# A ring of five in-place weight slots in a two-layer hybrid encoder, with every low part on VectorE and the memory's key and value units moved to the boundaries

## The chip, the cores and the metric

## The reference, cut to what matters

```python
for l in range(2):                       # x is (256, 1024), mem is (256, 1024), all float32
    x = layer_norm(ALPHA * x + 0.5 * swiglu(x, w_gate[l, 0], w_up[l, 0], w_down[l, 0]))   # d_ff 2816
    x = layer_norm(ALPHA * x + hybrid_mix(x))     # concat(diff attention, mLSTM, S5) @ w_out
    q, (k, v) = x @ wq[l], split(mem @ wkv[l])    # 4 heads of 256
    x = layer_norm(ALPHA * x + softmax(q @ k.T / 16) @ v @ wo[l])
    x = layer_norm(ALPHA * x + 0.5 * swiglu(x, w_gate[l, 1], w_up[l, 1], w_down[l, 1]))
```

The keys and values of the memory depend on `mem` and the weights alone, not on x.

## The kernel before

**Split products.** Each large product is made of three: both factors are split into a high part (`XH`, `WH`: a rounded copy, made by ScalarE) and a low part (`XL`, `WL`: the full number less the high part, made by VectorE's `low` or by GpSimd), and `prod` adds high x high, high x low and low x high into PSUM. 512 token-by-column results are 24 matmuls of 512 columns per unit, or 48 of 256.

**Units.** The weights come in units of 1 MB (128 partitions x 2048 float32), 99 a layer, in a fixed order: 33 for the first FFN (for each of 11 blocks two units of gate and up, one of down), K0, the mix's projections (DQ, SU, MQ, MK, DK, DV, MM), K1, K2, four units of V in the middle of the mix, five of `w_out` (the first two are half units), K3, four of `wq`, five of `wo` (two of them half), 33 for the second FFN. K and V are units of `wkv`, applied to the memory. A unit passes through slot u % 3 of three tiles, `RAW`, `WH` and `WL`. SyncE loads `RAW` (two transfers of 512 KB) when the low part of unit u - 3 is made (`load`); ScalarE's `split` waits for the load and until TensorE has used unit u - 3; VectorE's `split`, or for five units a layer (DQ1, the last two of `w_out`, the first of `wq`, the second of the second FFN) GpSimd's `split`, makes the low part; TensorE's `unit_ready` waits for that.

**Order.** Every engine's order is written out by hand, so that a low part stands at a fixed place between other steps of its engine and waits there. In the FFN, `step(j)` of ScalarE and VectorE makes H of block j high and low and the parts of three further units. In the mix, VectorE does the convolution and the S5 scans (`conv`, `s5_turn_in`), the masks and maxima (`diff_max`), the sums of the two softmaxes (`diff_combine`), the mLSTM sums and statistics (`mlstm_sums`, `mlstm_stats`) and the head norms (`diff_norm`); ScalarE the exponentials (`diff_exp`) and the copies out of PSUM (`diff_turned` copies the turned probabilities to AT). TensorE's memory units stand between the small matmuls of the heads.

**Boundaries.** Behind each of the four parts of a layer stands a boundary: VectorE's `norm_center` and `norm_scale` (a chain of small steps, `rsqrt`, in between), TensorE's `turn_x` turns the new X, ScalarE makes it high, VectorE low (`turned`). TensorE has one memory unit to do at the first boundary (K0) and at the second (K3), none at the third and fourth. At the first, third and fourth it starts the next product with tile 0 (128 tokens) alone; at the second, before the cross attention, it waits for both tiles.

**Loops.** The two layers are a hardware loop on each engine, and so are the blocks of the second FFN.

## Time and profile before

| | |
|---|---|
| median of 3 runs | 1379.81 us (1379.19 to 1384.34) |
| profiled execution | 1379.35 us |
| its span | 1377.7 us |
| busy: TensorE, VectorE, ScalarE, GpSimd | 92%, 62%, 42%, 17% |
| mean granted clock | 0.954 |
| transfers | 219.74 MB, 160 GB/s |

The span is the time from the first to the last instruction of the program; what lies around it is 1.65 us. Times in the rows count from the span's start. A row of the timeline is start, duration, engine, line, operation, output <- input, count, and in brackets the idle time of the engine ahead of it with what ended it. PE is TensorE, DVE VectorE, ACT ScalarE, POOL GpSimd.

### The profile page before, as it was taken

The page shows a single profiled execution, that of the slowest core. Times are in us where ns is not written, and L with a number is a line of the kernel's source. Part 1 is how long each engine was busy: PE and PEld are TensorE (multiplying, and loading weights), DVE is VectorE, ACT ScalarE, POOL GpSimd, SP SyncE. Part 2 cuts the span into 40 slices and gives each one's busy share as a digit, 9 for nine tenths or more (in the row PEclk, how much of TensorE's full clock was granted, in tenths as well). Part 3 has the DMA queues.
Part 4 walks back from the last instruction along what each step waited for, and adds up shares of the span by engine and source line. Part 5 has one row for each costly group of instructions (what it writes and reads, how often), then busy time and mean ns, then how long its engine had stood idle before and what let it go on. Part 6 is the DMA issues. An engine that isn't in the chain of part 4 may idle for free.

```text
span 1377.7 us, 18681 instructions
## 1 busy us (share of the span) xinstructions
PE 1267.3 (92%) x6376; PEld 1063.4 (77%) x6376; DVE 847.5 (62%) x1232; ACT 582.4 (42%) x659; POOL 232.1 (17%) x176
## 2 busy tenths in 40 slices
PE   5999997999978979999889999979997899899996
PEld 5877886978758868888768788868786797688885
DVE  4678556694875474445566774647758746645554
ACT  5443443435634444444354334434255244444442
POOL 0027001473040010000000440033902200000000
PEclk8999998999989989999989999989998899899999
DMA  8755553425234345555356555532433343455550
GB/s 274 269 174 183 188 177 105 135 97 178 92 123 152 128 145 196 192 193 183 124 202 208 183 184 183 183 123 93 153 107 123 108 153 123 155 190 192 192 185 30
DMA packets 151442, 219.74 MB, mean 160 GB/s; under 512 B 6720, under 2 KB 119488, under 8 KB 151104
## 3 DMA queue, kind: packets, MB, share of 16 engines
q1 hardware_dynamic: 148352, 205.61, 44.1%
q0 software_dynamic: 2736, 12.05, 2.4%
q8 instruction: 44, 0.72, 0.2%
q10 hardware_dynamic: 272, 1.05, 0.2%
q14 instruction: 38, 0.31, 0.1%
HBM read 217.63 MB, written 1.05 MB: 159 GB/s over the span
## 4 chain that ended last, share of the span: by engine, by line
PE 73%; DVE 18%; issue 6%; ACT 1%; DMA 1%; DVEq 0%; SPq 0%; ACTq 0%
PE PS L427 22%; PE PS L429 22%; PE PS L428 22%; DVE SM L1326 2%; DVE WL L1307 1%; DVE XG L1349 1%; PE PS L458 1%; DVE X L1343 1%; PE PS L496 1%; DVE ZS L1487 1%; DVE COUT L1499 1%; PE PS L900 1%; PE PS L924 1%; ACT WH L976 1%; DMA RAW<-in_ffn_w_up 1%
## 5 line engine op out<-in xcount | busy, mean ns | idle before, releaser
L1307 DVE TENSOR_TENSOR WL<-RAW,WH 128x2048 fp32r<-128x2048 f32 (+1 forms) x188 | 423.7, 2256 | 274.6 <-ACT WH L976 274.1
L976 ACT ACTIVATE WH<-RAW 128x2048 fp32r<-128x2048 f32 (+1 forms) x198 | 371.2, 1877 | 181.0 <-PE PS L429 178.8
L427 PE MATMUL PS<-WH,XH 128*128 128x512 f32 x832 | 337.6, 406 | 26.7 <-DVE XL L1307 20.2
L428 PE MATMUL PS<-WL,XH 128*128 128x512 f32 x832 | 330.4, 397 | 0.0
L429 PE MATMUL PS<-WH,XL 128*128 128x512 f32 x832 | 330.2, 397 | 0.0
L427 PEld LDWEIGHTS PS<-WH,XH 128*128 128x128 f32 x832 | 160.1, 192 | 62.3 <-issue 22.8
L429 PEld LDWEIGHTS PS<-WH,XL 128*128 128x128 f32 x832 | 159.9, 192 | 34.8
L428 PEld LDWEIGHTS PS<-WL,XH 128*128 128x128 f32 x832 | 160.6, 193 | 31.8
L427 PE MATMUL PS<-WH,HH 128*128 128x512 f32 x352 | 138.0, 392 | 4.0 <-DVE HL L1307 4.0
L429 PE MATMUL PS<-WH,HL 128*128 128x512 f32 x352 | 137.1, 389 | 0.0
L428 PE MATMUL PS<-WL,HH 128*128 128x512 f32 x352 | 137.0, 389 | 0.0
L1875 POOL TENSOR_TENSOR WL<-RAW,WH 128x2048 fp32r<-128x2048 f32 x10 | 45.6, 4561 | 342.8 <-ACT WH L976 342.8
L976 ACT ACTIVATE HH<-PS 128x512 fp32r<-128x512 f32 x44 | 26.3, 597 | 154.4 <-PE PS L458 154.4
L427 PEld LDWEIGHTS PS<-WH,HH 128*128 128x128 f32 x352 | 66.1, 188 | 19.9 <-issue 6.5
L1058 ACT ACTIVATE SG<-PS 128x256 f32<-128x256 f32 x88 | 33.8, 384 | 109.6 <-PE PS L429 109.5
L429 PEld LDWEIGHTS PS<-WH,HL 128*128 128x128 f32 x352 | 66.1, 188 | 13.9
L428 PEld LDWEIGHTS PS<-WL,HH 128*128 128x128 f32 x352 | 66.1, 188 | 13.4
L1307 DVE TENSOR_TENSOR HL<-PS,HH 128x512 fp32r<-128x512 f32 x44 | 30.4, 690 | 73.1 <-ACT HH L976 72.4
L427 PE MATMUL PS<-XH,WH 128*128 128x256 f32 x224 | 66.8, 298 | 3.2 <-DVE XL L1307 3.2
L428 PE MATMUL PS<-XL,WH 128*128 128x256 f32 x224 | 65.6, 293 | 0.0
L429 PE MATMUL PS<-XH,WL 128*128 128x256 f32 x224 | 65.3, 292 | 0.0
L496 PE MATMUL PS<-kst,X 128*128 128x128 f32 x128 | 24.4, 358 | 35.4 <-DVE X L1360 35.4
(308 smaller groups left out, 1796.0 us busy)
## 6 DMA issues: line engine op xcount, KB each, us to landing
RAW<-in_ffn_w_gate SPq DMA_DIRECT2D x88, 512.0 KB, 3.7
RAW<-in_ffn_w_up SPq DMA_DIRECT2D x88, 512.0 KB, 4.7
RAW<-in_ffn_w_down SPq DMA_DIRECT2D x88, 512.0 KB, 3.9
RAW<-in_w_in SPq DMA_DIRECT2D x44, 512.0 KB, 4.2
RAW<-in_xattn_wkv SPq DMA_DIRECT2D x32, 512.0 KB, 4.3
RAW<-in_xattn_wq SPq DMA_DIRECT2D x16, 512.0 KB, 4.3
RAW<-in_w_out SPq DMA_DIRECT2D x12, 512.0 KB, 3.9
RAW<-in_xattn_wo SPq DMA_DIRECT2D x12, 512.0 KB, 3.7
```

Source lines behind the costliest of these rows:

```text
L427: nc.tensor.matmul(out_ap, sh, mh, start=first, stop=False)
L428: nc.tensor.matmul(out_ap, sh, ml, start=False, stop=False)
L429: return nc.tensor.matmul(out_ap, sl, mh, start=False, stop=last)
L458: mm = nc.tensor.transpose(PS[:, 6, fc * SEQ + t * P:fc * SEQ + t * P + P], HB[:, t, fc * P:fc * P + P], ident)
L496: mm = nc.tensor.transpose(PS[:, 4 + 2 * t + half, i * P:i * P + P], X[:, t, c * P:c * P + P], ident)
L900: mm = nc.tensor.matmul(PS[:, h, t * SEQ:t * SEQ + SEQ], QX[:, 2 * h + c, t * P:t * P + P], KT[:, 2 * h + c, :], start=(c == 0), stop=(c = ...
L924: mm = nc.tensor.matmul(PS[:, 6 + h % 2, dc * SEQ:dc * SEQ + SEQ], V[:, mt, (2 * h + dc) * P:(2 * h + dc + 1) * P], XPT[:, h % 2, mt, :], ...
L976: return nc.scalar.activation(dst, src, ACT.Copy)
L1058: nc.scalar.activation(SG[:, t, :], PS[:, 4 + t, 0:FB], ACT.Silu).then_inc(sg_done.sem, 1)
L1307: return v.tensor_tensor(dst, full, hi.bitcast(F32), ALU.subtract)
L1326: ins = v.scalar_tensor_tensor(dst, a, 1.5, dst, ALU.add, ALU.mult)
L1875: g.tensor_tensor(WL[s][:, :], RAW[s][:, :], WH[s][:, :].bitcast(F32), ALU.subtract)\
```

## The change

- **Ring.** Five slots instead of three. A slot has `RAW` and `WH`; `WL` lies in the place of `RAW`, so the low part is written over the loaded unit. SyncE's load of unit u waits until TensorE has used unit u - 5. ScalarE's high part waits for the load alone. All low parts are on VectorE; GpSimd has none.
- **Place.** `split()` on ScalarE and VectorE takes the next unit of the order each time. Through the FFN and the mix it is one unit further on at the same place than before.
- **Memory units.** V units are eight column blocks of 256 with all 1024 rows (48 matmuls of 256 columns) instead of halves of the rows with 512 columns. `FILL` says where they are done: two at a boundary, four in the middle of layer 0's mix, none in layer 1's. Layer 1's K units are done at layer 0's last two boundaries.
- **Boundary.** Both tiles are centred and then scaled together everywhere. VectorE makes tile 0 of the turned X low, then the next weight's low part, then tile 1's.
- **Loops** are written out. The parameters come in four transfers instead of one, some of them in places that are free at that time; small rows of the gates lie in other tiles, and the heads' row maxima are spread by a column of the identity with stride 0 instead of a table.

```diff
-RING = 3
+RING = 5
+FILL = {("mix", 0): [(0, "K", 0), (0, "K", 1)],
+        ("mid", 0): [(0, "K", 2), (0, "K", 3), (0, "V", 0), (0, "V", 1)],
+        ("xattn", 0): [(0, "V", 2), (0, "V", 3)],
+        ("ffn2", 0): [(1, "K", 0), (1, "K", 1)],
+        ("next", 0): [(1, "K", 2), (1, "K", 3)],
+        ("mix", 1): [(1, "V", 0), (1, "V", 1)],
+        ("mid", 1): [],
+        ("xattn", 1): [(1, "V", 2), (1, "V", 3)],
+        ("ffn2", 1): [],
+        ("next", 1): []}
...
+EARLY = {(0, l): 2 for l in range(DEPTH)} | {(1, l): 2 for l in range(DEPTH)} | {(2, 0): 3, (2, 1): 1, (3, 0): 3, (3, 1): 0}
...
+        slots = [place(f"RAW{s}", [P, 2048], F32) for s in range(RING)]
+        RAW = [slot for slot, _ in slots]
+        WL = [sb(f"WL{s}", [P, 2048], F32R, at) for s, (_, at) in enumerate(slots)]
         WH = [sb(f"WH{s}", [P, 2048], F32R) for s in range(RING)]
-        WL = [sb(f"WL{s}", [P, 2048], F32R) for s in range(RING)]
...
-            def load(l, u, j, first, second):
-
-                sp.wait_ge(split_lo.sem, split_lo.at(l, u - RING + 1 + 3 * j))
+            def load(u, first, second):
+
+                if u >= RING:
+                    sp.wait_ge(unit_used.sem, u - RING + 1)
...
+            def memory_unit(key, b):
+
+                u = UNIT[key]
+                if key[1] == "K":
+                    form_b(u, b, MH, ML)
+                    return
+                unit_ready(u)
...
+                for t in range(TT):
+                    tok = slice(t * P, t * P + P)
+                    for c in range(KC):
+                        mm = prod(PS[:, b, t * 256:t * 256 + 256], MH[:, c, tok], ML[:, c, tok],
+                                  wh[:, c, :], wl[:, c, :], c == 0, c == KC - 1)
+                mm.then_inc(unit_used.sem, 1)
+
+            def fill(where, l):
+
+                for i, key in enumerate(FILL[where, l]):
+                    memory_unit(key, 7 - i)
...
# ScalarE
-                act.wait_ge(raw_loaded[s].sem, raw_loaded[s].at(l, 32 * (u // RING + 1) + 32 * j))
-                act.wait_ge(unit_used.sem, unit_used.at(l, u - RING + 1 + 3 * j))
+                act.wait_ge(raw_loaded[s].sem, 32 * (u // RING + 1))
                 copy(WH[s][:, 0:n], RAW[s][:, 0:n]).then_inc(split_hi.sem, 1)
...
+            def boundary(l, n):
...
                 square(l, n, 0)
                 square(l, n, 1)
...
+                fill_out(where, l, 0)
+                split()
...
+                turned(nl, nn, 0)
+                fill_out(where, l, 1)
+                turned(nl, nn, 1)
+                for i in range(EARLY[n, l] - 1):
+                    split()
...
# VectorE
+            def boundary(l, n):
...
+                norm_center(l, n, 0, last)
+                norm_center(l, n, 1, last)
+                norm_scale(l, n, 0, 2)
...
+                turned(nl, nn, 0)
+                split()
+                turned(nl, nn, 1)
+                for i in range(EARLY[n, l] - 1):
+                    split()
...
# VectorE, mix: the end, from the last decay_scores
                 diff_max(l, 4)
                 diff_max(l, 5)
...
                     CH[:, 6:8, :].rearrange("p f (k s) -> p f k s", s=2)).then_inc(c_lo.sem, 1)
+                split()
                 mlstm_sums(l)
-                split(l, U_WOUT[1], half=True)
                 diff_combine(l, 2)
+                split()
                 mlstm_stats(l)
                 diff_max(l, 6)
                 diff_max(l, 7)
-                split(l, U_WOUT[2])
+                split()
                 diff_combine(l, 3)
                 cat_low(l, 0, 4, 7)
                 diff_norm(l, 0)
                 cat_low(l, 1, 0, 4)
+                split()
                 diff_norm(l, 1)
                 cat_low(l, 2, 2, 5)
-                split(l, U_K[3])
+                split()
+                split()
...
# ScalarE, mix: the end
                 diff_exp(l, 4)
                 diff_exp(l, 5)
-                split(l, U_WOUT[1], half=True)
-                kv_out(l, 6)
-                kv_out(l, 7)
+                split()
+                if FILL["mid", l]:
+                    kv_out(FILL["mid", l][3], 0)
                 diff_evac(l, 1)
                 diff_turned(l, 2)
-                split(l, U_WOUT[2])
+                split()
                 diff_exp(l, 6)
                 diff_exp(l, 7)
-                split(l, U_WOUT[3])
+                split()
                 cat_high(l, 0, 4, 7)
...
# VectorE, end of the attention
                 output(3)
-                split(l, U_WO + 4)
-                split(l, U_FFN[1])
+                for i in range(4):
+                    split()
```

## Rows read from the trace of the kernel before

**Rows 1.** The page: busy time of the engines, and groups of instructions.
```profile
PE 1267.3 (92%) x6376; PEld 1063.4 (77%) x6376; DVE 847.5 (62%) x1232; ACT 582.4 (42%) x659; POOL 232.1 (17%) x176
...
L976 ACT ACTIVATE WH<-RAW 128x2048 fp32r<-128x2048 f32 (+1 forms) x198 | 371.2, 1877 | 181.0 <-PE PS L429 178.8
...
L1875 POOL TENSOR_TENSOR WL<-RAW,WH 128x2048 fp32r<-128x2048 f32 x10 | 45.6, 4561 | 342.8 <-ACT WH L976 342.8
```

**Rows 2.** Waits of TensorE, longest first: total us, times, longest.
```profile
PE PS L496 <- DVE X L1360: 35.4, 7, 6.5
PE PS L427 <- DVE XL L1307: 23.4, 8, 8.0
PE PS L724 <- DVE ES L1601: 13.4, 2, 6.7
...
PE PS L427 <- DVE HL L1307: 4.0, 4, 1.1
```

**Rows 3.** Groups of VectorE by form: busy us, mean ns, idle before.
```profile
L1307 DVE TENSOR_TENSOR WL<-RAW,WH 128x2048 fp32r<-128x2048 f32 x180 | 413.9, 2302 | 271.6 <-ACT WH L976 271.3
...
L1307 DVE TENSOR_TENSOR WL<-RAW,WH 128x1024 fp32r<-128x1024 f32 x8 | 9.8, 1223 | 3.1 <-ACT WH L976 2.8
```

**Rows 4.** Transfers: KB each, median us from issue to landing.
```profile
RAW<-in_ffn_w_up SPq DMA_DIRECT2D x88, 512.0 KB, 4.7
```

**Rows 5.** Windows: length, busy PE, PEld, DVE, ACT, POOL, clock, DMA, GB/s.
```profile
211.30:217.30 6.00, 5.96 (x49) 5.72 (x48) 5.58 (x16) 4.29 (x5) 0.00 (x0) 1.00 0.54 175
217.30:226.80 9.50, 1.97 (x8) 1.57 (x8) 8.38 (x7) 1.79 (x3) 4.50 (x1) 0.70 0.35 110
226.80:232.00 5.20, 5.17 (x15) 4.12 (x16) 0.00 (x0) 0.00 (x0) 0.00 (x0) 0.56 0.01 3
...
258.20:307.80 49.60, 46.47 (x256) 39.51 (x256) 48.61 (x66) 19.64 (x17) 28.25 (x21) 0.97 0.33 107
...
313.60:334.30 20.70, 20.70 (x153) 19.35 (x152) 7.68 (x10) 10.74 (x16) 9.92 (x11) 0.92 0.60 216
...
410.50:416.30 5.80, 5.80 (x49) 5.61 (x47) 5.63 (x9) 1.42 (x4) 1.46 (x1) 1.00 0.47 144
416.30:424.40 8.10, 3.47 (x17) 3.22 (x16) 6.63 (x15) 3.90 (x6) 1.12 (x2) 0.79 0.31 108
...
486.50:496.50 10.00, 1.99 (x9) 1.57 (x9) 9.39 (x10) 2.21 (x4) 4.02 (x1) 0.71 0.28 105
...
684.50:696.80 12.30, 2.02 (x10) 1.60 (x9) 11.02 (x24) 7.57 (x9) 0.00 (x0) 0.67 0.02 4
```

**Rows 6.** Timeline of the first boundary, VectorE and GpSimd.
```profile
217.34 0.16 DVE L1325 TENSOR_TENSOR SM<-SM 128x2 f32<-128x2 f32 x1
217.38 4.50 POOL L1875 TENSOR_TENSOR WL<-RAW,WH 128x2048 fp32r<-128x2048 f32 x1 [85.43 <-ACT WH L976]
217.53 4.36 DVE L1326 SCALAR_TENSOR_TENSOR SM<-SM 128x2 f32<-128x2 f32 x1
```

**Rows 7.** Timeline of layer 0's mix, VectorE and ScalarE.
```profile
363.32 0.17 DVE L1586 TENSOR_SCALAR SM<-SM 128x2 f32<-128x2 f32 x1
...
370.58 0.51 ACT L976 ACTIVATE AT<-PS 128x384 f32<-128x384 f32 x1
...
379.88 4.98 DVE L1601 SCALAR_TENSOR_TENSOR ES<-PR,SM,ES 128x128 f32<-128x128 f32 x2
...
388.53 4.42 DVE L1326 SCALAR_TENSOR_TENSOR SM<-SM 128x4 f32<-128x4 f32 x1
```

**Rows 8.** Timeline: ScalarE in the first FFN, VectorE behind the attention.
```profile
77.71 0.38 ACT L1058 ACTIVATE SG<-PS 128x256 f32<-128x256 f32 x1 [2.09 <-PE PS L429]
...
83.15 1.92 ACT L976 ACTIVATE WH<-RAW 128x2048 fp32r<-128x2048 f32 x1 [3.25 <-PE PS L429]
...
481.22 1.22 DVE L1343 SCALAR_TENSOR_TENSOR X<-PS,X 128x1024 f32<-128x1024 f32 x1 [1.30 <-PE PS L429]
```

**Rows 9.** Timeline of TensorE behind the last projection.
```profile
313.56 1.92 PE L654 MATMUL PS<-ZX,CQ 128*32 128x127 f32 x16
```

More of the change, by code:

```diff
@@ L67, with unit_order @@
-P_BT = 2290
-P_COLS = P_BT + 512
+RING = 5
+FFN_UNITS = 3 * BLOCKS
+FILL = {("mix", 0): [(0, "K", 0), (0, "K", 1)],
[5 rows of a table added]
+        ("mid", 1): [],
+        ("xattn", 1): [(1, "V", 2), (1, "V", 3)],
+        ("ffn2", 1): [],
+        ("next", 1): []}
+def unit_order():
+    order = []
+    for l in range(DEPTH):
+        order += [(l, "F0", i) for i in range(FFN_UNITS)]
+        order += FILL["mix", l]
+        order += [(l, "DQ", 0), (l, "DQ", 1), (l, "SU", 0), (l, "MQ", 0), (l, "MK", 0), (l, "DK", 0), (l, "DK", 1),
+                  (l, "DV", 0), (l, "DV", 1), (l, "MM", 0), (l, "MM", 1)]
+        order += FILL["mid", l]
+        order += [(l, "W", i) for i in range(5)]
+        order += FILL["xattn", l]
+        order += [(l, "WQ", i) for i in range(4)]
+        order += [(l, "WO", i) for i in range(5)]
+        order += FILL["ffn2", l]
+        order += [(l, "F1", i) for i in range(FFN_UNITS)]
+        order += FILL["next", l]
+    return order
@@ new lines, in load_single @@
+            def load_single(u, w, l, c):
+                r = raw(u)
+                load(u, (r[:, 0:512], w[l, c, :, 0:512]), (r[:, 512:1024], w[l, c, :, 512:1024]))
+            def load_ffn(l, s):
+                load_gu(l, s, 0, 0, 0)
+                load_gu(l, s, 1, 0, 1)
+                for j in range(BLOCKS - 1):
+                    load_gu(l, s, 2 + 3 * j, j + 1, 0)
+                    load_gu(l, s, 3 + 3 * j, j + 1, 1)
+                    load_down(l, s, 4 + 3 * j, j)
+                load_down(l, s, FFN_UNITS - 1, BLOCKS - 1)
@@ L385, in _, with load_fill @@
+            def load_fill(where, l):
+                for kl, kind, i in FILL[where, l]:
+                    load_cols(UNIT[kl, kind, i], wkv_v, kl, 256 * i + (D if kind == "V" else 0))
+            for l in range(DEPTH):
                 load_ffn(l, 0)
-                load_cols(l, U_K[0], wkv_v, 0)
+                load_fill("mix", l)
                 for half in range(2):
-                    load_rows(l, U_DQ + half, win_v, 4 * half, 4, slice(C_DQ, C_DQ + 512))
-                load_cols(l, U_SU, win_v, C_SU)
@@ L490, in turn_x @@
                 for half in range(2):
-                    if n in (1, 2) and t == 1 and half == 1:
-                        pe.wait_ge(kv_read.sem, kv_read.at(l, 1 if n == 1 else 8))
+                    if t == 1:
+                        fill_read(("next", "mix", "xattn", "ffn2")[n], l - 1 if n == 0 else l, 1 - half)
                     for i in range(4):
@@ L965, in _ @@
                     mm.then_inc(xT_psum.sem, 1)
-            with pe.Fori(0, DEPTH) as l:
+            for l in range(DEPTH):
                 ffn(l, 0)
@@ L1280, in _ @@
                     .then_inc(xT_hi.sem, 1)
-            with act.Fori(0, DEPTH) as l:
+            split()
+            turned(0, 0, 0)
+            split()
+            turned(0, 0, 1)
+            split()
+            split()
+            for l in range(DEPTH):
                 ffn(l, 0)
-                split(l, U_DQ)
-                boundary(l, 0, U_FFN[0] + 32)
+                boundary(l, 0)
                 mix(l)
-                boundary(l, 1, U_WOUT[4])
+                boundary(l, 1)
                 xattn(l)
-                boundary(l, 2, U_WO + 4)
+                boundary(l, 2)
                 ffn(l, 1)
-                square(l, 3, 0)
-                square(l, 3, 1)
+                boundary(l, 3)
+            assert next(units, None) is None
         @block.vector
@@ L1834, in _ @@
                     MH[:, 4 * half:4 * half + 4, t * P:t * P + P]).then_inc(xT_lo.sem, 1)
-            with dve.Fori(0, DEPTH) as l:
+            split()
+            turned(0, 0, 0)
+            split()
+            turned(0, 0, 1)
+            split()
+            split()
+            for l in range(DEPTH):
+                count["n"] = 0
                 layer["l"] = l
```

717 lines of the change are left out of this document (337 added, 380 removed).

## The prediction

> **What bounds the kernel now.** I read the page first, then TensorE's waits, then windows and timelines where it waits. TensorE is busy 92% of the span, VectorE 62%, ScalarE 42% [rows 1]: the products bound the kernel, and a change can win what TensorE waits, plus what its clock loses behind a wait. The waits [rows 2] are few and long: 35.4 us for the normalised X, 23.4 for the low part of the turned X, 13.4 for the probabilities of the mix. So the four boundaries of a layer and the mix can move, the FFNs hardly. A weight unit costs ScalarE 1.9 us (high part) and VectorE 2.3 (low part; half a unit 1.2) or GpSimd 4.6 [rows 1, 3]; TensorE 5.7 in 256-column matmuls (the 5.7 us of K0 between 211.5 and 217.3 [rows 5]), 5.4 in 512-column ones.
>
> **The stall that goes.** GpSimd's low part runs from 217.38 for 4.50 us, and the small VectorE step that starts at 217.53 lasts 4.36; the step before it, alone, takes 0.16 [rows 6]. So a GpSimd low part holds VectorE 4.2 us. There are five a layer; four meet the chain, this one, two in the mix (4.98, 4.42 [rows 7]) and one behind the attention. The change removes all ten and VectorE pays 10 x 2.3 = 23 us. Whether those lie on the chain decides. The Trainium skill, "GPSIMD Engine Reference", Key points, says that GpSimd shares its SBUF interfaces with VectorE and contends with instructions with two SBUF inputs. By that rule, the trace agrees.
>
> **Boundaries with two units under them.** Before the mix: the last FFN product ends at 211.5, one unit fills to 217.3, TensorE waits 6.0, turns X at low clock (2.0) and starts the next product 1.6 later, at 226.8; its first tile takes 5.1 us at clock 0.56 [rows 5], where twelve such matmuls take 2.7 at full clock. In all 15.3 + 2.4 = 17.7. After: two units 11.5, turning 1.0, the same 1.6: 14.1. The norm under it needs 1.2 + 0.3 + 1.3 + 2.4 (twelve steps of 0.2) + 1.3 = 6.5, hidden by the units; with one unit alone as cover it would show 0.8. So -3.6, twice: **-7.2**, and a unit more is done each time. After layer 0's second FFN 12.3 + 2.4 = 14.7 becomes 14.1: **-0.6**, with two units done. After layer 0's attention 10.0 + 2.4 = 12.4 [rows 5] becomes 14.1: **+1.7**, with two units done. Should the 1.6 alone bring the low clock, each of the five is 2.4 worse; after 1.6 us alone no row shows it.
>
> After layer 1's attention nothing fills, and four low parts stand in VectorE's queue ahead of the norm. The last one's load starts when the third WO unit is used, 5.4 before the norm may begin, and needs two issues and 4.7 to land [rows 4], 5.0 in all; then 1.9 and 2.3: VectorE is free 3.4 later than at 481.2 [rows 8]. From 484.6, both tiles centred (2.8 + 2.8), 2.5, scaled 1.3, turned, high and low 3.6: 497.6, where the stalled version started at 496.5. **+1.0**.
>
> **Boundary before the cross attention.** There TensorE starts only when both tiles are low. Before: 5.8 of one unit, then 8.1 [rows 5], 13.9. After: units 11.5, tile 0 turned 1.0, its high 0.7 and low 0.8, then a whole weight's low part, 2.3, ahead of tile 1's low, 1.4: 17.8 with the gaps. Tile 1's turning also waits for ScalarE's copy of the second unit, which stands behind tile 0's high; the 2.3 covers it. **+3.9, twice: +7.8**; without the low part in between, 2.3 less each.
>
> **The mix.** From 258.2 to 307.8 VectorE is busy 48.61 of 49.60 us [rows 5], with the same steps in the same order after; nothing moves. Behind that, layer 0 loses two of six memory units and layer 1 all six. They were cover, not path: TensorE works on one while VectorE works towards the next combine. And each low part stands a place earlier, so that one waits for a high part that ScalarE makes only after copying AT, which waits for TensorE, which waits for VectorE's combine. Layer 0 in times of before, from the last step of the sixth maximum (ended 363.5 [rows 7], now 362.3 since a half low part replaces a whole one): exponentials 0.8, high 1.9, low 2.3, sums 2.4, combine 1.7 give 371.4. Turn 0.6, AT 0.5 [rows 7], high 1.9, low 2.3: 376.7. Statistics 4.0, masks and maxima 2.9: 383.6. Exponentials 0.9, high 1.9, low 2.3, combine 1.7: 390.4, where it was 384.9 with its stall. Low 0.7, norm 4.5 (8.7 before, with the stall of 4.42): 395.6. Turn, high, low 2.0, weight's low 2.3, norm 4.5: 404.4, was 400.6. Turn 0.6, half a unit 2.7, a unit 5.4: 413.1, against 410.5 [rows 5]. That is +2.6, with 0.9 for low clock behind the longer waits **+3.5**. Bounds: if neither low part waits for ScalarE, 3.0 and 2.8 less, so -3; if the last three units run at half clock, +8 on top.
>
> Layer 1, without any unit: from the last projection (307.9) the same steps reach the sixth maximum 15.6 us sooner at full clock, since they then follow each other without a unit of 5.4 to 5.7 in between; with the +2.6, and 1.2 that this stretch took longer in layer 1 before, -14.2. But for 60 us TensorE has only small matmuls. With units still between, the clock is 0.92 from 313.6 to 334.3 [rows 5]. The small groups on the path are 1.9 [rows 9], three turns 1.8, spread 2.0, scores 2.2 and 1.1, output 0.9: 9.9 us at full clock and as much again at half, so -4.7 at half clock throughout. I take **-8**, between the ends but nearer half.
>
> **First FFN.** TensorE waits 4.0 us in four waits for the low part of H [rows 2], behind VectorE's preparation, which queues behind a low part whose high part began at 83.15, when a unit was used [rows 8]. In the ring it waits for a load released one unit earlier, at 77.7 [rows 8], landed 5.0 later: 0.45 won, and at the next one, where TensorE's own wait lay between, all of 0.9: -1.3, twice: **-2.6**. Elsewhere a load must be landed, high and low in 5.0 + 1.9 + 2.3 = 9.2 us and has four units, 22 us: the load's wait for TensorE's use, and the loads queued behind it on SyncE, cost nothing, unless loads take over 17 us. GpSimd issues four parameter transfers instead of one in the first block, of about the same bytes, read only after that block.
>
> **Sum.** -7.2 - 0.6 + 1.7 + 1.0 + 7.8 + 3.5 - 8 - 2.6 = -4.4. The profiled execution took 1379.35 us, 1.65 outside its span of 1377.7, and lies 0.5 below the median shown. 1379.35 - 4.4 = **1375**, 0.35% below the median. A measurement of this kernel can tell about 0.5%, 6.9 us, from no change: this is none.
>
> **Rivals.** (a) *The clock stays up in layer 1's mix*: -14.2 in place of -8: 1369. For it: between 258.2 and 307.8, with small matmuls among the units, the clock was 0.97 [rows 5]. Against: no unit is left. 0.25. (b) *The low parts cost nothing where the stalls go*: eight stalls of 4.2 on the chain go, VectorE's new low parts find gaps, the mix of layer 0 gains its two (its -3 for my +3.5), and the cross attention's boundary hides its 2.3 twice: 1375 - 6.5 - 4.6 = 1364. For it: 4.36 against 0.16 [rows 6]. Against: the queue order of the walk. 0.12. This is the page's rule with nothing given back. (c) *Slower: the low clock outlasts the waits*. If TensorE stays at 1.2 GHz from the third combine through the output units in both layers, the last two and a half units take 5.4 to 8 us more in each (13 together), the small matmuls of layer 1 take the 3.3 that I left out: 1391. It decides once the low clock reaches the last output units. For it: 5.1 instead of 2.7 behind every long wait [rows 5]. Against: the clock came back within one tile each time. 0.18. My own case has 0.45.
>
> **Chances and range.** Below 1372.9: (b), most of (a), a fifth of mine: 0.40. Above 1386.7: most of (c): 0.17. Between: 0.43. Range 1361 to 1389, which leaves out the far ends of (b) and (c); my own case runs from 1368 to 1383.
>
> **What would show it.** No GpSimd step of 4.5 us and no small VectorE step over 2 us beside one. One wait of 1.6 us behind the turned X at the four mix and FFN boundaries with units, at full clock. Before the cross attention a wait near 3 us for tile 1's low part, with a weight's low part between the tiles'. In layer 0's mix VectorE waiting twice for ScalarE's high part, and the last output unit 2 to 4 us later, counted from the last projection. In layer 1 a granted clock of 0.5 to 0.7 over some 60 us, and the stretch about 8 us shorter. I am wrong if that clock is full, if those low parts do not wait, or if a load comes late anywhere.

## The result: within what the measurement tells, on the slow side

The changed kernel takes 1385.06 us in the median of 20 runs, the kernel before 1379.96: a ratio of 1.0029, 95% interval 1.0019 to 1.0040. The interval lies wholly above 1, so the kernel is slower, by 0.3%, which is less than the 0.5% that the prediction called no change. The prediction was 1375 (range 1361 to 1389, with a chance of 0.43 for a time that counts as no change). The time lies in the range, but the prediction had the kernel faster and it is slower. The profiled execution has a span of 1381.2 us (1383.08 us in all), 3.5 more than before, where the sum had said -4.4.

The page of the changed kernel, busy times and the two costliest groups of the vector engines (against [rows 1]):

```profile
PE 1267.2 (92%) x6568; PEld 1072.4 (78%) x6568; DVE 825.9 (60%) x1218; ACT 577.4 (42%) x656; POOL 184.0 (13%) x172
...
L1373 DVE TENSOR_TENSOR WL<-RAW,WH 128x2048 fp32r<-128x2048 f32 (+1 forms) x198 | 445.3, 2254 | 267.1 <-ACT WH L1040 267.0
L1040 ACT ACTIVATE WH<-RAW 128x2048 fp32r<-128x2048 f32 (+1 forms) x198 | 370.3, 1876 | 149.1 <-DMA RAW<-in_ffn_w_up 129.5
```

VectorE does ten low parts more and is still busy 21.6 us less: the stalls under GpSimd's low parts counted as busy time. TensorE does the same work and is busy as long as before. Its waits (against [rows 2]):

```profile
PE PS L782 <- DVE ES L1659: 30.9, 6, 8.5
PE PS L466 <- issue: 10.5, 6, 2.6
PE PS L466 <- DVE WL L1373: 9.4, 2, 4.7
PE PS L466 <- ACT XH L1040: 7.9, 5, 1.6
PE PS L534 <- DVE X L1429: 7.5, 1, 7.5
PE PS L466 <- DVE XL L1373: 6.8, 1, 6.8
```

The wait for the normalised X went from 35.4 us to 7.5. That for the turned X stood under its low part (XL) with 23.4 us before, 8.0 of them at the program's start; now the start's 6.8 us are all that is left under XL, and the waits behind the turned X stand in two other rows: five of some 1.6 us under its high part (XH), 7.9 in all, and two of 2.6 us before the cross attention under "issue", whose row also holds the first FFNs' waits of 2.35 and 2.15. At the boundaries this makes 50.8 us before and 23.3 now (with two of 1.3 us at the second tile's turning). The wait for the probabilities of the mix (ES) grew from 13.4 to 30.9, and all waits in the two mixes from 29 to 60. What left the boundaries came back in the mix. The windows by stage, in the order of the columns of [rows 5]:

```profile
212.90:226.90 14.00, 12.38 (x105) 12.17 (x104) 8.87 (x22) 5.62 (x9) 0.00 (x0) 1.00 0.58 178
226.90:232.00 5.10, 5.10 (x27) 4.32 (x28) 3.12 (x3) 1.67 (x3) 0.00 (x0) 1.00 0.38 133
305.80:415.80 110.00, 87.25 (x502) 74.80 (x503) 66.03 (x162) 47.85 (x83) 16.01 (x16) 0.84 0.26 87
415.80:433.20 17.40, 13.45 (x113) 13.03 (x111) 11.92 (x25) 8.11 (x10) 1.11 (x2) 0.98 0.61 212
433.20:440.00 6.80, 6.80 (x35) 6.80 (x36) 2.15 (x1) 0.00 (x0) 0.00 (x0) 0.56 0.01 2
497.90:511.90 14.00, 12.38 (x105) 12.17 (x103) 9.54 (x22) 6.29 (x9) 1.04 (x2) 1.00 0.86 266
995.90:1090.70 94.80, 67.17 (x310) 53.18 (x311) 56.95 (x158) 40.52 (x75) 13.91 (x16) 0.77 0.20 67
1171.60:1182.60 11.00, 2.00 (x9) 1.59 (x9) 9.71 (x22) 5.42 (x7) 1.05 (x2) 0.72 0.48 174
```

The boundaries with two units (first and sixth row) and the first tile behind them (second row) do what was forecast: 14.0 us, full clock. The mix of layer 0 (third row) has a clock of 0.84: since the clock has two levels, 2 x (1 - 0.84) = 32% of its 110 us ran at 1.2 GHz. In layer 1's mix (0.77) it is 46%.

All stages, from TensorE's timeline (from the first to the last product named), with two experiments beside them: all low parts on VectorE and nothing else changed, and the same with idle matmuls at the boundaries, the fastest kernel:

| stage, us | before | changed | low parts alone | fastest |
|---|---|---|---|---|
| start to end of first FFN, layer 0 | 211.5 | 212.9 | 211.9 | 212.5 |
| to first product of the mix | 15.3 | 14.0 | 10.4 | 10.4 |
| to the last projection (MM1) | 81.1 | 78.9 | 81.8 | 79.0 |
| MM1 to last `w_out` unit | 102.7 | 110.0 | 100.8 | 100.7 |
| to first product of the attention | 13.9 | 17.4 | 13.0 | 11.9 |
| attention | 62.1 | 64.7 | 62.1 | 62.1 |
| to second FFN | 10.0 | 14.0 | 5.7 | 5.7 |
| second FFN | 188.0 | 185.9 | 188.7 | 188.7 |
| to layer 1's first FFN | 12.2 | 14.0 | 12.1 | 12.3 |
| first FFN, layer 1 | 193.5 | 191.2 | 193.7 | 192.6 |
| to the mix | 15.3 | 14.0 | 10.4 | 10.4 |
| to MM1 | 81.3 | 78.9 | 80.6 | 79.0 |
| MM1 to last `w_out` unit | 103.8 | 94.8 | 99.5 | 97.8 |
| to the attention | 14.1 | 17.4 | 13.0 | 11.9 |
| attention | 63.7 | 63.5 | 62.1 | 62.1 |
| to second FFN | 10.0 | 11.0 | 5.7 | 5.7 |
| second FFN | 188.3 | 187.8 | 188.7 | 188.7 |

### The profile page after: what moved, and what is told of

It reads as the page before. It is cut to its first block, busy times and chain, and to the rows that moved or that the text cites. A ratio compares the mean times of both kernels' runs of the same rounds, so it can differ in the third digit from the quotient of the medians.

```text
span 1381.2 us, 15974 instructions
## 1 busy us (share of the span) xinstructions
PE 1267.2 (92%) x6568; PEld 1072.4 (78%) x6568; DVE 825.9 (60%) x1218; ACT 577.4 (42%) x656; POOL 184.0 (13%) x172
## 4 chain that ended last, share of the span: by engine, by line
PE 79%; DVE 12%; ACT 3%; issue 3%; POOL 2%; DMA 1%; SPq 0%; DVEq 0%; POOLq 0%
PE PS L466 24%; PE PS L467 24%; PE PS L468 24%; DVE WL L1373 3%; PE PS L497 1%; ACT WH L1040 1%; DMA RAW<-in_ffn_w_up 1%; DVE COUT L1557 1%; DVE ZS L1545 1%; PE PS L534 1%; PE PS L961 1%; PE PS L985 1%; ACT XH L1040 1%; POOL RO L1994 1%; ACT PR L1157 1%
## 5 line engine op out<-in xcount | busy, mean ns | idle before, releaser
L1373 DVE TENSOR_TENSOR WL<-RAW,WH 128x2048 fp32r<-128x2048 f32 (+1 forms) x198 | 445.3, 2254 | 267.1 <-ACT WH L1040 267.0
L466 PE MATMUL PS<-WH,XH 128*128 128x512 f32 x832 | 333.0, 400 | 24.1 <-DVE WL L1373 9.4
L467 PE MATMUL PS<-WL,XH 128*128 128x512 f32 x832 | 327.1, 393 | 0.0
L1458 DVE TENSOR_TENSOR HB<-SG,PS 128x256 f32<-128x256 f32 x88 | 36.2, 417 | 32.6 <-ACT SG L1115 32.4
L466 PE MATMUL PS<-WH,CH 128*128 128x512 f32 x128 | 55.3, 432 | 0.0
```

Source lines behind the costliest of these rows:

```text
L466: nc.tensor.matmul(out_ap, sh, mh, start=first, stop=False)
L467: nc.tensor.matmul(out_ap, sh, ml, start=False, stop=False)
L1373: return v.tensor_tensor(dst, full, hi.bitcast(F32), ALU.subtract)
L1458: v.tensor_tensor(HB[:, t, :], SG[:, t, :], PS[:, 4 + t, FB:2 * FB], ALU.mult).then_inc(h_ready.sem, 1)
```

## The experiments

Each ratio is to the kernel before, with its 95% interval; where an experiment edits the changed kernel, it is to be compared with that kernel's 1.0029. Stage times are from one profiled execution each, as above. In the changed kernel and the experiments on it, the same boundaries come out alike to 0.1 us where no edit touches them (14.0 and 17.4; 11.0 to 11.4 behind layer 1's attention). Other stages that no edit touches differ more: layer 0's mix takes 110.0 to 112.3 us, the first FFN 212.2 to 214.6 in layer 0 and 191.2 to 194.5 in layer 1, layer 0's attention 63.3 to 64.7. A difference of 2 us in one of these shows nothing by itself.

### One part alone: all low parts on VectorE

In the kernel before, GpSimd's five low parts a layer are given to VectorE; slots, units and fillings stay.

```diff
                 turned(l, n + 1, 0)
+                if n == 0:
+                    split(l, U_DQ + 1)
                 if n == 2:
+                    split(l, U_FFN[1] + 1)
                     norm_scale(l, n, 1, 2)
...
                 cat_low(l, 0, 4, 7)
+                split(l, U_WOUT[3])
                 diff_norm(l, 0)
                 cat_low(l, 1, 0, 4)
+                split(l, U_WOUT[4])
                 diff_norm(l, 1)
                 cat_low(l, 2, 2, 5)
                 split(l, U_K[3])
+                split(l, U_WQ)
```

> The kernel before with one part of the change alone: the five low parts a layer of GpSimd are VectorE's, in the order of the units (between the tiles of the turned X at the first and third boundary, the others in the last part of the mix); three slots, units and fillings stay. Theory A, the prediction's (a GpSimd low part holds a VectorE step 4.2 us, on the chain at the first and third boundary): from the last FFN product to the first product of the mix 15.3 us become 9.2 to 10, with 2.4 us more where the low clock goes too; behind the attention 10.0 become 7 to 8; the two stalls in the mix go for low parts of 2.3: the kernel gains 15 to 22 us. Rival B (the step of VectorE was not the last thing that the turning waited for, or the low parts that it gets instead stand ahead of something on the path): gains of under 1 us a boundary, the mix 2 to 4 us longer, the kernel within 5 us.

Measured: 0.9800 (0.9779 to 0.9822), a span of 1350.8: -26.9 us, more than Theory A allowed. The windows of the first boundary, the mix of layer 0, and the boundary behind its attention:

```profile
211.90:222.20 10.30, 6.79 (x56) 6.35 (x54) 9.63 (x22) 5.82 (x8) 0.00 (x0) 0.96 0.31 99
...
304.00:404.80 100.80, 92.66 (x502) 76.13 (x503) 66.62 (x162) 49.63 (x84) 16.07 (x16) 0.94 0.40 136
...
479.90:485.60 5.70, 1.11 (x10) 0.88 (x9) 5.16 (x8) 2.21 (x4) 0.00 (x0) 0.89 0.00 0
```

The first boundary is 4.9 us shorter with its one unit, the one behind the attention 4.3, both about the length of a stall (4.2). So this part of the change was worth 27 us by itself, and the rest of it, on top, costs 1381.2 - 1350.8 = 30.4.

The table shows where. The seven boundaries hold 12 memory units in place of 4 and are 31.5 us longer. Layer 0's mix has two units fewer and is yet 9.2 longer; layer 1's, with none of its six, is only 4.7 shorter. The other stages give back 5.8. No run has the five slots without the other parts, so what the slots alone are worth is open.

### The stall put back by a subtraction that nobody needs

The kernel above, with this on GpSimd behind the attention:

```diff
+                pool.wait_ge(split_hi.sem, split_hi.at(l, U_FFN[1] + 2))
+                pool.wait_ge(y_half.sem, y_half.at(l, 3))
+                pool.sem_inc(waits_apart.sem, 1)
+                g.tensor_tensor(KT[:, :, :], MH[:, :, :].bitcast(F32), ML[:, :, :].bitcast(F32), ALU.subtract)
```

> The kernel before with all low parts on VectorE, and one idle subtraction of 128 x 2048 on GpSimd between tiles that nobody needs then, behind the attention of both layers, while VectorE does the norm; nothing waits for it. Theory A (a GpSimd operation with two operands in the same memory holds VectorE's small step whatever the data): one of VectorE's steps takes 4.3 to 4.5 us and the boundary of 5.7 us 9.9 to 10.1. Rival B (the long step of VectorE in the kernel before waited for the low part itself, by order or address): no step grows, the boundary stays at 5.7.

Measured: 0.9833 (0.9810 to 0.9855). The timeline of GpSimd and of VectorE in that kernel:

```profile
477.43 4.50 POOL L2017 TENSOR_TENSOR KT<-MH,ML 128x2048 f32<-128x2048 f32 x1 [63.74 <-ACT WH L976]
```

```profile
477.53 4.41 DVE L1326 SCALAR_TENSOR_TENSOR SM<-SM 128x1 f32<-128x1 f32 x1
```

A one-column step takes 4.41 us, and the boundary 9.92 us in place of 5.68: Theory A, in both layers (4.42 and 9.93 in layer 1). No data link the two operations, and VectorE waits for nothing of GpSimd's there. By the Trainium skill, "GPSIMD Engine Reference", Key points, GpSimd contends with VectorE instructions that have two SBUF inputs; the step held has two, and the trace agrees.

### The low parts of the mix one place later

```diff
                     CH[:, 6:8, :].rearrange("p f (k s) -> p f k s", s=2)).then_inc(c_lo.sem, 1)
-                split()
                 mlstm_sums(l)
...
                 cat_low(l, 2, 2, 5)
                 split()
                 split()
+                split()
```

> The changed kernel, with each of VectorE's low parts in the last part of the mix one place later (none ahead of the mLSTM sums, three at the end, as many as before in all). Theory A, that of the prediction (a low part one place early waits for a high part that ScalarE makes only behind the copy of AT or behind the exponentials): the three idle times of VectorE ahead of a low part, 2.3 + 3.3 + 2.9 = 8.5 us in layer 0, go nearly whole, the third combine ends 4.5 us sooner and the fourth 8 to 11; each layer's stretch from the last projection to the last output unit is 7 to 10 us shorter, the kernel 14 to 20. Rival B (TensorE's own work and its low clock bound that stretch, VectorE only fills it): the two stretches together lose less than 4 us. Rival C: the low part that is moved to the end is missed by the last output unit or by the norm, and gives 2.3 us back in each layer: 9 to 15.

The changed kernel's VectorE in layer 0's mix:

```profile
362.52 0.69 DVE L1373 TENSOR_TENSOR CL<-UT,CH 128x512 fp32r<-128x512 f32 x1
365.46 2.29 DVE L1373 TENSOR_TENSOR WL<-RAW,WH 128x2048 fp32r<-128x2048 f32 x1 [2.25 <-ACT WH L1040]
...
375.19 2.29 DVE L1373 TENSOR_TENSOR WL<-RAW,WH 128x2048 fp32r<-128x2048 f32 x1 [3.32 <-ACT WH L1040]
...
387.68 2.29 DVE L1373 TENSOR_TENSOR WL<-RAW,WH 128x2048 fp32r<-128x2048 f32 x1 [2.85 <-ACT WH L1040]
```

and its ScalarE:

```profile
372.86 0.49 ACT L1040 ACTIVATE AT<-PS 128x384 f32<-128x384 f32 x1 [6.68 <-PE PS L782]
373.25 1.90 ACT L1040 ACTIVATE WH<-RAW 128x2048 fp32r<-128x2048 f32 x1
```

The copy of AT waits for TensorE, the high part stands behind it, VectorE's low part behind that, and so the next maxima. With the edit:

```profile
307.40:405.40 98.00, 83.81 (x502) 72.02 (x503) 64.75 (x161) 46.62 (x81) 18.11 (x16) 0.91 0.29 97
986.20:1073.70 87.50, 70.38 (x310) 55.98 (x311) 56.02 (x158) 39.88 (x74) 13.94 (x16) 0.75 0.22 72
```

Measured: 0.9867 (0.9853 to 0.9882). Layer 0's stretch goes from 110.0 to 98.0 us, layer 1's from 94.8 to 87.5: 19.3 in all, at the upper end of Theory A, with layer 0 above it. The span of this execution, 1364.3 us, is 16.9 shorter, since its first FFNs, which the edit does not touch, are 1.6 and 2.1 longer; it is the slowest of the kernel's four executions. In layer 0 the gain is more than the 8.4 us of VectorE's waits; the clock rose from 0.84 to 0.91 with it.

### The low clock in the mix

Idle matmuls (512 columns, 0.226 us each, into a bank that nobody reads) ahead of waits. First in layer 1's mix, at the boundaries before the attention and behind layer 1's:

```diff
+            def warm(b, n):
+                for i in range(n):
+                    nc.tensor.matmul(PS[:, b, :], MH[:, 0, 0:P], MH[:, 0:2, :].rearrange("p c n -> p (c n)"),
+                                     start=True, stop=True)
...
                 turn_x(l, 2, 0)
+                warm(0, 4)
                 turn_x(l, 2, 1)
+                warm(0, 10)
...
```

> The changed kernel with idle matmuls of 512 columns (into a bank that nobody reads) where TensorE waits: 8, 12 and 33 ahead of the three long waits of layer 1's mix, 30 behind layer 1's attention, 4 and 10 at both boundaries before the cross attention. They add work on TensorE of 0.226 us each at full clock and change no other engine. Theory A (the low clock behind waits costs what the prediction charged): behind layer 1's attention the turning and the first tile lose 1.0 + 2.0 us, the first projection of the attention 3.4 and 1.7, layer 1's mix, half of which runs at 1.2 GHz, 4 to 6: the kernel gains 10 to 14. Rival B: the matmuls are late themselves and push what stands behind them, and the clock falls elsewhere: within 3 us of the changed kernel. Rival C: in the mix VectorE and ScalarE set the pace, so that only the boundaries gain: 5 to 8.

Measured: 1.0014 (1.0003 to 1.0025), 1.2 us under the changed kernel's span. The attention took 62.1 in both layers (-2.6, -1.5) at full clock. Layer 1's mix took 94.0 at 0.84 instead of 94.8 at 0.77, so 14 us less of low clock brought 0.8. Behind layer 1's attention the product started 0.7 us later, and its first matmuls ran at low clock all the same. This is closest to Rival B, with the attention as an exception.

Then in layer 0's mix:

> The changed kernel with idle matmuls in four waits of layer 0's mix (11, 33, 11 and 16 of 0.226 us). There 34 of 110 us run at low clock. Theory A (low clock is what this stretch costs beyond the prediction, which had 3.5 us for it and the waits and measured 7.3): the low clock goes down to under 15 us, and the stretch from 110.0 to 106 or less. Rival B (as in layer 1's mix, where 14 us less of low clock brought 0.9: VectorE and ScalarE set the pace and TensorE's small matmuls only follow): 109 to 111.5.

Measured: 1.0046 (1.0029 to 1.0063); the time is not shorter, the stage is:

```profile
306.30:413.90 107.60, 97.14 (x573) 82.56 (x574) 65.77 (x162) 47.92 (x82) 16.02 (x16) 0.94 0.27 89
```

The low clock went from 34 to 13 us and the stage from 110.0 to 107.7, between the two expectations. As untouched executions of this stage lie between 110.0 and 112.3, the 21 us of low clock were worth 2 to 5. Both edits together:

> The changed kernel with the low parts of the mix's end one place later and idle matmuls in the first two waits of layer 0's mix (11 and 15, as the second wait is 4 us long there). Apart, the places took layer 0's stretch from 110.0 to 98.0 us and its low clock from 34 to 17 us, the idle matmuls took it to 107.7 and 13. Theory A (the low clock and the low parts' waits are costs of their own): 95.5 to 97. Theory B (the low clock there was a result of VectorE's waits and cost what it did only through them): 98.

Measured: 0.9853 (0.9828 to 0.9879). Layer 0's stage took 99.0 us at 0.91, the clock it had without idle matmuls: they changed nothing there. But layer 1's mix, which no edit of this kernel touches beyond the one before, took

```profile
987.50:1068.50 81.00, 62.71 (x310) 49.49 (x311) 54.38 (x155) 39.27 (x73) 13.96 (x16) 0.86 0.24 78
```

81.0 us at 0.86 where it had taken 87.5 at 0.75. From 44 to 23 us of low clock (2 x (1 - clock) x length), 6.5 us less: a third of the difference. The two kernels as wholes do not differ (0.9853 and 0.9867, with intervals that overlap), and the four executions of the one without idle matmuls differ by as much among themselves: spans from 1357.3 us at a mean clock of 0.969 to 1364.3 at 0.962, 7.0 us for some 19 of low clock. So where the low clock falls differs between executions of one kernel, and the time goes with it, a third of the low clock. That the low clock causes all of this time, and whether the time at which the stage starts decides, is not shown.

### Parameter transfers one unit later

```diff
-                pool.wait_ge(unit_used.sem, UNIT[l, "F0", 0] + 1)
+                pool.wait_ge(unit_used.sem, UNIT[l, "F0", 1] + 1)
```

> The changed kernel, with GpSimd's six parameter transfers issued when the second unit of the first FFN is used, not the first. Theory A (the load is late): in the changed kernel the ring's load of the sixth unit and these transfers are issued within 0.3 us of each other, the load takes 11 us, and ScalarE's high part of it stands ahead of the high part of H; TensorE then waits 2.3 us in layer 0 and 2.2 in layer 1, and layer 0 runs at low clock for 3.4 us behind that wait. With the transfers 2.7 us later both waits go, and the time falls by 2.3 + 1.7 + 2.2 = 6.2 us. Rival B (the order alone does it: the high part of a unit ahead of H costs its 1.9 us whenever it runs): the waits stay at 1 to 2 us and the time falls by less than 2. Rival C: the preparation on VectorE now waits for the parameters and TensorE waits a block later: no change within 1 us.

The changed kernel, in this order: SyncE's queue, GpSimd's queue, ScalarE.

```profile
29.18 0.38 SPq L374 DMA_DIRECT2D RAW<-in_ffn_w_gate  x1
```

```profile
29.46 0.53 POOL L2047 DMA_DIRECT2D PAR<-in_params  x1 [18.93 <-PE PS L468]
...
32.09 0.53 POOL L1934 DMA_DIRECT2D LNGB<-in_ln_b  x1
```

```profile
40.64 1.92 ACT L1040 ACTIVATE WH<-RAW 128x2048 fp32r<-128x2048 f32 x1 [8.35 <-DMA RAW<-in_ffn_w_up]
42.46 0.58 ACT L1040 ACTIVATE HH<-PS 128x512 fp32r<-128x512 f32 x1
```

In the kernel before, where the same load is issued at 29.62 and the parameters' transfer at 30.70, ScalarE makes H high ahead of this unit:

```profile
38.64 0.60 ACT L976 ACTIVATE HH<-PS 128x512 fp32r<-128x512 f32 x1 [3.69 <-PE PS L458]
39.13 1.91 ACT L976 ACTIVATE WH<-RAW 128x2048 fp32r<-128x2048 f32 x1
```

ScalarE in the changed kernel with the edit:

```profile
33.60 1.92 ACT L1040 ACTIVATE WH<-RAW 128x2048 fp32r<-128x2048 f32 x1 [2.40 <-DMA RAW<-in_ffn_w_up]
36.70 0.60 ACT L1040 ACTIVATE HH<-PS 128x512 fp32r<-128x512 f32 x1 [1.18 <-PE PS L497]
```

Measured: 0.9993 (0.9983 to 1.0003). The load of the sixth unit took 11.4 us; now it takes 5.5 and lands 7 sooner, H is high 5.8 sooner, and the first FFNs are 4.3 and 2.0 us shorter: Theory A. The order on ScalarE stays as it was, so it is the late load, and not the order alone, that cost the time. The kernel's ratio is 5 us under the changed kernel's.

### The low part behind both tiles, before the attention

```diff
                 turned(nl, nn, 0)
-                split()
+                if n != 1:
+                    split()
                 turned(nl, nn, 1)
+                if n == 1:
+                    split()
```

> The changed kernel, with the weight's low part behind both tiles of the turned X at the boundary before the cross attention alone. The prediction priced the low part between the tiles at 2.3 us in each layer. Theory A (so it is, nothing else is late): the wait for tile 1 falls from 2.6 to 0.3, 4.6 us in all. Theory B (ScalarE's high part of tile 1 ends 1.85 us ahead of VectorE's low part and is itself behind the copy of the second memory unit): VectorE can start 1.7 and end 1.1 us sooner, the kernel gains 2.2. Theory C: the first projection waits for the weight's low part instead: no gain.

Measured: 1.0007 (0.9999 to 1.0016), 3 us under the changed kernel. The boundary goes from 17.4 to 16.4 us in both layers: Theory B, as far as the boundary goes. In the changed kernel the low part between the tiles runs from 429.59 to 431.87, but ScalarE starts tile 1's two high parts only here:

```profile
430.14 1.08 ACT L1040 ACTIVATE XH<-PS 128x512 fp32r<-128x512 f32 x2 [0.81 <-PE PS L534]
```

So tile 1's low part can't start before 430.7 nor end before some 431.9, where it ended at 433.1. The attention behind it ran at full clock and took 62.05 us, which is a gain of another 2.6 and 1.5 us that none of the theories had.

### The norm behind layer 1's attention

One low part moved from ahead of the norm to behind it:

```diff
                 output(3)
-                for i in range(4):
+                for i in range(4 if l == 0 else 3):
                     split()
...
                 turned(nl, nn, 1)
-                for i in range(EARLY[n, l] - 1):
+                for i in range(EARLY[n, l] - (0 if (n, l) == (2, 1) else 1)):
                     split()
```

> The changed kernel with VectorE's fourth low part behind layer 1's attention moved from ahead of the norm to behind the turned X. Theory A, the prediction's (nothing fills there and the norm stands behind these low parts): from the last attention product to the first of the FFN 11.0 us become 8.7, the 7.5 us wait for X is 2.3 shorter. Rival B (the norm waits for TensorE's half of the last units or for ScalarE anyway): no change there, and the FFN's first block waits for the moved low part: the same or 1 us slower.

Measured: 1.0057 (1.0038 to 1.0076). The boundary took 9.9 us instead of 11.0, half of what Theory A had, and the kernel as a whole was not faster than the changed one. With the norm by tiles as well:

```diff
+                tiles = (n, l) == (2, 1)
                 norm_center(l, n, 0, last)
+                if tiles:
+                    norm_scale(l, n, 0, 1)
                 norm_center(l, n, 1, last)
-                norm_scale(l, n, 0, 2)
+                if not tiles:
+                    norm_scale(l, n, 0, 2)
...
                 turned(nl, nn, 0)
+                if tiles:
+                    norm_scale(l, n, 1, 2)
                 split()
```

> The changed kernel with layer 1's boundary behind the attention as in the kernel before (tile 0 scaled ahead of tile 1's centring, tile 1 scaled behind tile 0's low part) and one low part fewer ahead of the norm. Theory A (of the 5.3 us that this boundary takes longer than in the kernel with all low parts on VectorE, 11.0 against 5.7, nearly all is the scaling of both tiles together, since one low part fewer brought 1.1): 11.0 become 6 to 7.5. Rival B (the low parts ahead of the norm and their loads set it): 9.5 to 10.

Measured: 1.0009 (0.9993 to 1.0024). The boundary took 7.7 us, just above Theory A's range and well under Rival B's: of the 5.3 us to the kernel with all low parts on VectorE, 3.3 are found. The last 2.0 were not tried apart.

### The edits together, and the units elsewhere

> The changed kernel with the three edits that moved a stage of it together (parameter transfers one unit later, low parts of the mix's end one place later, the weight's low part behind both tiles before the cross attention) and the idle matmuls at that boundary alone. Theory A (the edits touch stages of their own and add): the stages measured apart give -4.3 and -2.0 in the first FFNs, -12.0 and -7.3 in the mixes, -1.0 twice at the boundary and -2.6 and -1.5 in the attention behind it: 31.7 us under the changed kernel, a span of 1349 to 1352 us. Rival B (the clock takes part back: each time that falls away is one in which TensorE stood, but the low clock moves elsewhere): 1353 to 1360.

Measured: 0.9822 (0.9800 to 0.9845), a span of 1353.0, 28.2 of the 31.7 us: they nearly add. Layer 0's mix gave 10.1 of its 12.0. With all these repairs the changed kernel stands where the kernel before stands with its low parts on VectorE alone (1350.8).

Then one unit in place of two at four boundaries:

```diff
-        ("ffn2", 0): [(1, "K", 0), (1, "K", 1)],
-        ("next", 0): [(1, "K", 2), (1, "K", 3)],
-        ("mix", 1): [(1, "V", 0), (1, "V", 1)],
-        ("mid", 1): [],
-        ("xattn", 1): [(1, "V", 2), (1, "V", 3)],
+        ("ffn2", 0): [(1, "K", 0)],
+        ("next", 0): [(1, "K", 1)],
+        ("mix", 1): [(1, "K", 2)],
+        ("mid", 1): [(1, "K", 3), (1, "V", 0), (1, "V", 1), (1, "V", 2)],
+        ("xattn", 1): [(1, "V", 3)],
...
```

> The kernel of the run before this one with one memory unit instead of two at four boundaries (behind both FFNs of layer 0 and layer 1's first FFN and mix), the four others in layer 1's mix, at the places of layer 0's. Theory A (of two units at a boundary the second is path, since the norm needs 6.6 us and one unit is 5.8): each of the four boundaries is 4.8 us shorter, 14.0 to 9.2 and 16.4 to 11.6; the four units in layer 1's mix cost what they cost in layer 0, (98.0 - 87.5) / 4 = 2.6 us each: the kernel gains 19.2 - 10.5 = 8.7 us. Rival B (with less work ahead, the low clock comes back behind the norm, 2.4 us a boundary, and the units in the mix are path): 0 to 3 us slower or the same.

Measured: 0.9861 (0.9840 to 0.9882), 2.4 us above the span of the run before. The boundaries fell to 10.1 to 10.4 (from 14.0) and 12.2 (from 16.9), 16.1 in all; the stages behind the three of 14.0 grew by 1.6 to 3.0 with low clock in them, 6.2 together; and layer 1's mix took 12.9 more, 3.2 a unit. That is Rival B: a unit of some 5.7 us of work costs about 2.5 net at a boundary and 3.2 in the mix.

### Idle matmuls at the boundaries, on the kernel with all low parts on VectorE

The idle matmuls are seven on either side of the turning before the mix, 8 and 6 before the attention, 26 behind the second FFN, 24 transposes at the first turning of the first FFN, 4 and 14 ahead of the second FFN.

> The kernel before with all low parts on VectorE (the fastest so far, a span of 1350.8 us), and idle matmuls into a bank that nobody reads wherever TensorE waits at a boundary: 0.226 us each, a little less of them than fills the wait. Theory A (the low clock behind a boundary follows TensorE's standing still, and is path there): in that kernel DQ to the fifth-last projection takes 81.8 and 80.6 us with 6.7 at low clock where the changed kernel's takes 78.9 without, the second FFN 188.7 where the changed kernel's takes 185.9, the first FFN of layer 1 another 2.4; the idle matmuls give back 1.7 to 2.9 at each of six places and 1 us of the turning: 12 to 16 us. Rival B (they do not hold the clock through the last 1.6 us wait, as behind layer 1's attention in the run with 30 of them, where it fell all the same and the product started 0.7 later): within 3 us.

Measured: 0.9745 (0.9726 to 0.9764), 6.7 us less of span: half of Theory A. The projections went to 79.0 us in both layers and the boundary before the attention to 11.9, but the second FFNs grew to 190.2. The next kernel leaves out the matmuls ahead of them:

> The kernel with all low parts on VectorE and idle matmuls, without the 4 and 14 of them ahead of the second FFN, where they took a wait of nothing and moved it 2.5 us long behind the second tile's turning (190.2 us for that FFN in place of 188.7). Theory A: 1.5 us less in each layer, 3.0 in all. Theory B (without them the low clock that they kept off comes back and costs as much): within 1 us of it.

Measured: 0.9737 (0.9714 to 0.9761), 1343.56 us in the median of five, the fastest. The second FFNs are back at 188.7, as Theory A has it; the span fell by 2.2. Its two mixes, the same instructions:

```profile
301.80:402.50 100.70, 92.48 (x502) 76.05 (x503) 66.60 (x161) 49.65 (x84) 16.12 (x16) 0.94 0.40 136
964.90:1062.70 97.80, 89.72 (x502) 74.48 (x503) 67.06 (x161) 49.64 (x84) 18.16 (x16) 0.97 0.40 140
```

In the run before, the layers had it the other way round, 97.8 in layer 0 and 100.6 in layer 1.

## Why the prediction was wrong, by its own steps

| step | predicted | measured |
|---|---|---|
| boundaries before the mix, with the clock behind them | -3.6, -3.6 | -3.5, -3.7 |
| after layer 0's second FFN | -0.6 | -0.6 |
| after layer 0's attention | +1.7 | +1.9 |
| after layer 1's attention | +1.0 | +1.0 |
| before the cross attention | +3.9, +3.9 | +3.5, +3.3 |
| the cross attention itself | 0 | +2.6, -0.2 |
| layer 0's mix | +3.5 | +7.3 |
| layer 1's mix | -8 | -9.0 |
| first FFNs | -1.3, -1.3 | +1.4, +0.1 |
| second FFN of layer 1 | 0 | -0.5 |
| sum | -4.4 | +3.6 (spans: +3.5) |

(Where a boundary's row counts the low clock of the first tile, 2.4 us, the measured value is that of boundary and stage together; behind layer 0's second FFN 2.4 us of the next stage's gain are put to the boundary, the rest to layer 1's first FFN.)

The sum missed by 8.0 us: 4.1 in the first FFNs, 3.8 in layer 0's mix and 2.4 in the attention on one side, 2.3 in other steps on the other. That the time lies in the range all the same is no merit of the sum.

**What held.** The seven boundaries came out within 0.6 us each. Their mechanism, stall out and a second unit in, is shown by the run with the stall put back and by the one with the low parts alone. The low part between the tiles before the attention, though, was priced at 2.3 and costs 1.0: ScalarE's high part is the later one. Layer 1's mix came within 1.0 us, with a clock of 0.68 over the 58 us from 1012.6. Two slips in the working changed nothing: behind layer 1's attention its own terms give 5.0 + 1.9 + 2.3 - 5.4 = 3.8 where it has 3.4 (the norm did begin 3.8 us later against the last product), and in layer 1's mix -14.2 + 9.9 is -4.3 and not -4.7.

**First FFN, 4.1 us off.** "Elsewhere a load must be landed, high and low in 5.0 + 1.9 + 2.3 = 9.2 us and has four units, 22 us" is the step that failed. The two waits for the low part of H in each layer did go, but for 0.5 us in layer 0. But the load of the sixth unit has not 22 us, since its high part now stands ahead of H's on ScalarE. It is issued at 29.18, and H is ready to be made high at 37.8; less the 1.9 of the high part, it has 6.7 us to land. It took 11.4, since it is issued within 0.3 us of the parameter transfers (before: 1.1) and they share the transfer engines, whose share is 1.04 from 32 to 44 us; the text had counted only their bytes. TensorE waits 2.35 and 2.15 us for it, with low clock behind the wait in layer 0. Moving the transfers took both waits away. The prediction had named the sign of this itself: it is wrong "if a load comes late anywhere".

**Layer 0's mix, 3.8 us off.** The mechanism was right: low parts wait for ScalarE's high parts. Three sizes were not, and the times of VectorE and TensorE tell them apart.

```profile
341.77 0.56 DVE L1640 TENSOR_TENSOR ES<-PS,kst 128x384 f32<-128x384 f32 x1 [4.11 <-PE PS L771]
...
404.39 1.14 DVE L1678 SCALAR_TENSOR_TENSOR CAT<-CAT,SM,PAR 128x128 f32<-128x128 f32 x4
```

First, 2.1 us were counted twice. The full clock at the mix's first products was booked as won to the end, and MM1 did start 2.1 us sooner, at 305.8; but it stood behind a wait of 4.7 us instead of 3.2, VectorE's maxima began only 0.4 sooner (341.77 against 342.13), and the sixth maximum ended at 362.6, where the walk in times of before has 362.3. Second, VectorE ended the last norm at 405.5, 1.1 us behind the walk's 404.4. Third, the last step, from that norm to the last output unit, is 8.7 us in the walk, 10.0 in the kernel before and 10.2 in the changed one: 1.5 more. Less the 0.9 booked for low clock this is the 3.8.

The low clock was mis-sized too: booked with 0.9 us, it covers 34 us of the stage, and keeping 21 of them away took 2 to 5 us off. And the low parts' waits, of which the bounds had two, at 3.0 and 2.8 us, were worth far more: all three low parts one place later gave 10.1 to 12.0 us. What is left then, -2.8 to -4.7 to the kernel before, is about the -3 that the prediction gave for a mix in which neither low part waits.

**Attention, 2.4 off.** The low clock behind the waits of 1.3 and 2.6 us covers the first projection in layer 0 (0.56 in the window from 433.2). The sum had nothing for it; both runs that shortened or filled the last wait are free of it. In six other executions with this boundary as it is, the stage took 63.3 to 63.6, so that 1.4 of the 2.6 is what it mostly costs. Layer 1 shows no loss because the kernel before had it there already (63.7 against 62.1).

**The comparison that was missing.** The forecast netted each boundary's stall against its second unit and never asked what the stall's removal is worth by itself. It is 27 us. Rival (b) came nearest, with 1364, but as a luckier course of the same kernel, where it was a kernel of its own.

## What to carry to other kernels

Price every part of a bundled change by itself before netting: here one part gave 27 us and the others took 30 back. An order written by hand one place further ahead makes an engine wait for its producer's queue, so check for each moved step what stands ahead of its producer. Count the time that a load has only up to the first step that stands behind its consumer in an engine's queue (here 7 us, not 22), and list which transfers are issued in the same microseconds.

## What was not expected of the hardware

The same instructions of the mix took 97.8 and 100.7 us in the two layers of one execution, at a granted clock of 0.97 and 0.94, and 81.0 and 87.5 us in two kernels, at 0.86 and 0.75. With 6 us more at the low level the stage was 3 us longer where TensorE was busy 92% of it. With 21 us more it was 6.5 longer where TensorE was busy 80%, and 2 to 5 longer in layer 0's mix of the changed kernel. By the Trainium skill, "TensorE: Matmul & The Clock Gate", Terms, time at a clock that passes K of N pulses costs about (1 - K/N) of itself, which at 1.2 of 2.4 GHz is half: the first case agrees, and the other two lie under it.

Thirty idle matmuls did not keep the clock up for the product behind layer 1's attention, where two waits of 2.2 and 1.6 us followed them, while 4 and 10 closer to the product before the attention did.
